# Divided weights, x in quarters, queries blanked to 128 rows: one edit of a two-block transformer kernel on one Trainium2 core

## The chip, the core and the metric

The kernel runs on one core of one Trainium2 chip. A core has five engines that work side by side: PE (TensorE, matrix products), DVE (VectorE, elementwise work and sums), ACT (ScalarE, functions of one operand with a scale), POOL (GpSimd) and SP (SyncE, which here issues the DMAs). Each runs its own instructions in order; semaphores hold one engine back until another has done something. Products land in PSUM, everything else lies in SBUF. The metric is the time of one execution on the device in microseconds (us); noise is small: the runs of this kernel lie within 0.02% of each other.

## The reference

Two blocks follow each other, both on 256 tokens of width 1024, float32. Cut to what matters:

```python
def first_block(x, ...):
    h = x + 0.5 * swiglu(rmsnorm(x, ffn1_norm), ffn1_w_gu, ffn1_w_down)
    u = rmsnorm(h, mix_norm)
    qa, ka, va, qb, kb, vb, qi, ki, wi, g = split(u @ w_in)      # 8 + 8 heads of 64
    qa, ka, qb, kb = (rmsnorm(z, its gain of 64) for z in (qa, ka, qb, kb))
    out_a = dsa_attention(qa, ka, va, qi, ki, wi, bias_dsa)      # the 64 best keys
    out_b = moba_attention(qb, kb, vb, bias_moba)                # one block of 256: causal
    g_a, g_b = split(sigmoid(g + b_gate))
    h = h + (g_a * (out_a @ w_branch_dsa) + g_b * (out_b @ w_branch_moba)) @ w_out
    return h + 0.5 * swiglu(rmsnorm(h, ffn2_norm), ffn2_w_gu, ffn2_w_down)

def second_block(x, mem, ...):                                   # two layers
    for i in range(2):
        a = rmsnorm(h, norm_mix[i])
        h = h + (mla_mixer(a) if i == 0 else stick_breaking_mixer(a))
        h = h + mem_cross_attn(rmsnorm(h, norm_cross[i]), rmsnorm(mem, norm_mem[i]))
        h = h + square(relu(rmsnorm(h, norm_mlp[i]) @ w_in)) @ w_out
    return rmsnorm(h, norm_final)

def mem_cross_attn(h, m, w_q, w_kv, w_o):                        # 4 heads of 128, 256 keys
    p = softmax(q @ k.T * 128 ** -0.5)
    return (p @ v) @ w_o
```

The mla mixer has 8 causal heads: scores contract 128 + 64 numbers, values have 128. Its output also goes through a softmax whose sum can be divided out before or after the product with the values.

## The kernel before, in words

**Products.** Each float32 factor is split into a high part, which one pass of PE takes exactly, and a low part. `mm3` makes one product of three matmuls, L394 (high by high), L395 and L396 (each with one low part). Weights stream in chunks by SP's DMAs into a ring of four buffers `w_raw`; ACT writes a chunk's high part `whi` (L351), DVE the low part `wlo` (L359), and a chunk is used once PE has waited for both (`take_chunk`). `next_hi(n)` and `next_lo(n)` split the chunk four places on in the plan, so ACT and DVE stand at most a ring ahead of PE.

**Phases.** A list of phases is walked by each engine in the same order: ffn1, the projections of the first mixer, its attention (`Attend`), mixture, ffn2, mla down, up, attend and out, a norm phase, the memory attention (`CrossAttention`), mlp, the second mixer (sb_in, stick, sb_out), and norm, memory attention, mlp and the final norm again. The order inside of a phase is written out by hand.

**A norm** before a projection is not applied to the rows: x is transposed on PE (L428) in four pairs of 128 columns, ACT writes the pair's high part `xt_h` with the gain (L441), DVE the low part `xt_l` (L494), and the root of the mean square, found meanwhile by ACT (L450) and DVE (L469 to L478), scales the outcome later. `norm_tensor`, `norm_scalar` and `norm_vector` do two pairs (one half) each.

**The opening.** x lands in three pieces (256, 256 and 512 columns) between the first chunks. Chunk 0, two tiles of 512 columns, is split tile by tile (L367, L374), chunks 1 to 3 whole. PE transposes pairs 0 and 1, multiplies with chunk 0, transposes pairs 2 and 3, and goes on with chunks 1, 2 and 3 (`up`), chunk c holding k = 2c and 2c + 1, two row tiles t each. L773 is the product of gate and up that frees the accumulator.

**Attention.** `Attend` works in groups of up to 512 score columns. For each, PE multiplies queries and keys (`score`, L1353), DVE adds the bias and finds the negated maximum (`log_vector`, L1450), ACT takes exp with the row's sum (L1430), PE transposes the weights (`turn`, L1362), DVE copies them (`copy_vector`, L1439), PE multiplies with the values (`value`, L1373). At the end of a row tile `out_rows` (DVE, L1299, L1300) divides by the sum, `fin.turn` (PE, L1312) transposes the rows, and `take_hi`, `take_lo` (L1325) split them for the next projection. Fillers stand between the groups: for the first mixer the gates' products, for mla the memory's keys and values (`keys0`, `values0`); their `groups` say after which group each step stands. In the first mixer two heads of 64 share the 128 partitions of `qt` and `kt`; a score matmul takes the half of one head, and a group holds heads of the same half:

```python
half = slice(64 * (hd % 2), 64 * (hd % 2) + 64)
qk=[(qt[half, k4, t * P:(t + 1) * P], kt[half, k4, 0:keys])]
```

`CrossAttention` has the same steps for 4 groups, in an order of its own, between the queries' projection and `project` (the output's). `memory` makes it, and `mem_groups` its groups.

**Tails.** `tail_scalar` and `tail_vector` order, at the end of an output projection, the splits of the coming chunks, the residual's additions and the following norm. A feed-forward network has the same in its own `tail`, and `Project` copies a unit's outcome out of PSUM (`copy_out`, L1000 for sb).

## Time and profile before

| | us |
|---|---|
| median of 3 runs | 1296.85 (1296.83 to 1296.98) |
| the profiled execution | 1297.06 |
| its span on the core | 1295.2 |
| PE busy | 1267.4 (98%) |
| DVE busy | 761.2 (59%) |
| ACT busy | 651.4 (50%) |

The span runs from the first to the last recorded instruction; the 1.86 around it are start and end of the program. The granted clock of TensorE over the span was 0.998 of full speed. Rows of the timeline further below name an engine, a line of the kernel, the operation with its output and input, shapes, and in brackets how long the engine was idle before and which work of another engine ended that. Runs of like instructions are one row, whose start is that of the first and whose time is busy time. Matmul records overlap: a matmul of 512 columns is busy for 0.39 but the next starts 0.23 later, so costs are read from starts.

### The profile page before, as it was taken

What the parts mean: (1) busy time and instruction counts of PE and PEld (TensorE: products, weight loads), DVE (VectorE), ACT (ScalarE), POOL (GpSimd) and SP (SyncE); (2) the same over time, 40 slices, a digit from 0 to 9 for tenths busy, and PEclk for the clock granted to TensorE, in tenths of its full rate; (3) what the DMA queues carried; (4) which work ended last, traced back from release to release, by engine and by line L of the source; (5) the groups of instructions that cost most, each with busy time, mean ns of one, the idle gap of its engine ahead of it and who ended that gap; (6) DMA issues with size and microseconds to landing.
All of it is one profiled execution on the core that took longest, in us unless ns stands there. A gap on an engine that the chain in (4) does not pass through costs nothing.

```text
span 1295.2 us, 16841 instructions
## 1 busy us (share of the span) xinstructions
PE 1267.4 (98%) x6766; PEld 1084.2 (84%) x6766; DVE 761.2 (59%) x1089; ACT 651.4 (50%) x836; POOL 18.1 (1%) x22
## 2 busy tenths in 40 slices
PE   8999999999999999999999999999999999999997
PEld 6888888888888888888888799999787887889896
DVE  6554548887676555448755575554644655754544
ACT  6454447564355444437945464443555744643432
POOL 0000000001000000000000000000000000000001
PEclk9999999999999999999999999999999999999999
DMA  8755546544443655534723175554474332655540
GB/s 289 284 192 183 187 144 231 210 147 153 157 147 133 221 189 196 188 133 152 267 70 126 66 257 183 181 193 130 164 258 163 109 103 82 224 199 182 192 131 33
DMA packets 39213, 221.72 MB, mean 171 GB/s; under 512 B 4485, under 2 KB 5141, under 8 KB 23648
## 3 DMA queue, kind: packets, MB, share of 16 engines
q1 hardware_dynamic: 36672, 214.20, 47.8%
q0 software_dynamic: 1024, 4.22, 1.0%
q10 hardware_dynamic: 1440, 2.22, 0.7%
q8 instruction: 54, 0.88, 0.3%
q14 instruction: 23, 0.19, 0.0%
HBM read 219.55 MB, written 1.07 MB: 170 GB/s over the span
## 4 chain that ended last, share of the span: by engine, by line
PE 88%; DVE 7%; ACT 3%; issue 1%; DMA 1%; SPq 0%; ACTq 0%; DVEq 0%
PE ps L394 22%; PE ps L396 22%; PE ps L395 22%; PE ps L603 4%; PE ps L605 4%; PE ps L604 4%; DVE wlo L359 3%; PE ps L1353 2%; PE ps L1373 2%; ACT whi L351 1%; PE ps L955 1%; PE ps L1362 1%; PE ps L428 1%; PE ps L636 1%; ACT xt_h L441 1%
## 5 line engine op out<-in xcount | busy, mean ns | idle before, releaser
L359 DVE TENSOR_TENSOR wlo<-w_raw,whi 128x2048 fp32r<-128x2048 f32 (+4 forms) x244 | 468.3, 1927 | 381.6 <-ACT whi L351 381.2
L351 ACT ACTIVATE whi<-w_raw 128x2048 fp32r<-128x2048 f32 (+4 forms) x244 | 393.4, 1618 | 427.5 <-PE ps L396 323.4
L394 PE MATMUL ps<-whi,xt_h 128*128 128x512 f32 (+3 forms) x784 | 308.5, 394 | 4.9 <-DVE xt_l L494 1.7
L396 PE MATMUL ps<-whi,xt_l 128*128 128x512 f32 (+3 forms) x784 | 302.8, 386 | 0.0
L395 PE MATMUL ps<-wlo,xt_h 128*128 128x512 f32 (+3 forms) x784 | 302.2, 385 | 0.0
L394 PE MATMUL ps<-whi,ot_h 128*128 128x512 f32 x594 | 235.7, 397 | 0.5 <-DVE ot_l L785 0.5
L396 PE MATMUL ps<-whi,ot_l 128*128 128x512 f32 x594 | 232.1, 391 | 0.0
L395 PE MATMUL ps<-wlo,ot_h 128*128 128x512 f32 x594 | 231.8, 390 | 0.0
L394 PEld LDWEIGHTS ps<-whi,xt_h 128*128 128x128 f32 x784 | 147.3, 188 | 38.6 <-issue 8.0
L396 PEld LDWEIGHTS ps<-whi,xt_l 128*128 128x128 f32 x784 | 147.2, 188 | 29.4
L395 PEld LDWEIGHTS ps<-wlo,xt_h 128*128 128x128 f32 x784 | 147.5, 188 | 27.1
L603 PE MATMUL ps<-xt_h,whi 128*128 128x256 f32 x512 | 145.6, 284 | 3.2 <-DVE xt_l L494 1.8
L605 PE MATMUL ps<-xt_l,whi 128*128 128x256 f32 x512 | 145.2, 284 | 0.0
L604 PE MATMUL ps<-xt_h,wlo 128*128 128x256 f32 x512 | 145.2, 284 | 0.0
L396 PEld LDWEIGHTS ps<-whi,ot_l 128*128 128x128 f32 x594 | 111.6, 188 | 23.7
L394 PEld LDWEIGHTS ps<-whi,ot_h 128*128 128x128 f32 x594 | 111.7, 188 | 22.7 <-issue 1.2
L395 PEld LDWEIGHTS ps<-wlo,ot_h 128*128 128x128 f32 x594 | 111.8, 188 | 21.5
L603 PEld LDWEIGHTS ps<-xt_h,whi 128*128 128x128 f32 x512 | 98.3, 192 | 4.9 <-issue 4.4
L604 PEld LDWEIGHTS ps<-xt_h,wlo 128*128 128x128 f32 x512 | 98.3, 192 | 0.5
L605 PEld LDWEIGHTS ps<-xt_l,whi 128*128 128x128 f32 x512 | 98.3, 192 | 0.0
L441 ACT ACTIVATE xt_h<-ps,gain 128x256 fp32r<-128x256 f32 x88 | 34.3, 478 | 45.0 <-PE ps L428 45.0
L494 DVE SCALAR_TENSOR_TENSOR xt_l<-ps,gain,xt_h 128x256 fp32r<-128x256 f32 x88 | 36.4, 477 | 23.1 <-ACT xt_h L441 23.1
(205 smaller groups left out, 878.3 us busy)
## 6 DMA issues: line engine op xcount, KB each, us to landing
w_raw<-ffn_mid SPq DMA_DIRECT2D x80, 768.0 KB, 4.3
w_raw<-mlp_mid SPq DMA_DIRECT2D x56, 1024.0 KB, 5.0
w_raw<-w_qkv SPq DMA_DIRECT2D x12, 1024.0 KB, 5.0
w_raw<-w_sb_qkv SPq DMA_DIRECT2D x12, 1024.0 KB, 5.1
w_raw<-w_xkv SPq DMA_DIRECT2D x8, 1024.0 KB, 5.0
w_raw<-ffn_first SPq DMA_DIRECT2D x8, 512.0 KB, 4.1
w_raw<-w_gate_b SPq DMA_DIRECT2D x4, 1024.0 KB, 5.0
w_raw<-w_gate_a SPq DMA_DIRECT2D x4, 1024.0 KB, 4.8
```

Source lines behind the costliest of these rows:

```text
L351: nc.scalar.activation(whi[:, s, 0:tiles * width], w_raw[:, s, 0:tiles * width], ACT.Copy).then_inc(w_hi, 1)
L359: nc.vector.tensor_tensor(wlo[:, s, 0:tiles * width], w_raw[:, s, 0:tiles * width], whi[:, s, 0:tiles * width].bitcast(F32), ALU.subtract) ...
L394: nc.tensor.matmul(acc, hi, whi[:, s, c], start=start, stop=False)
L395: nc.tensor.matmul(acc, hi, wlo[:, s, c], start=False, stop=False)
L396: return nc.tensor.matmul(acc, lo, whi[:, s, c], start=False, stop=stop)
L441: last = nc.scalar.activation(to[:, k], bank[:, j * S:(j + 1) * S], ACT.Copy, scale=gain[:, 8 * NORM[name] + k:8 * NORM[name] + k + 1])
L494: last = nc.vector.scalar_tensor_tensor(out=lo[:, k], in0=bank[:, j * S:(j + 1) * S], scalar=g, in1=hi[:, k].bitcast(F32), op0=ALU.mult, o ...
L603: nc.tensor.matmul(acc, whi[:, s, c], xt_h[:, k], start=k == 0, stop=False)
L604: nc.tensor.matmul(acc, wlo[:, s, c], xt_h[:, k], start=False, stop=False)
L605: last = nc.tensor.matmul(acc, whi[:, s, c], xt_l[:, k], start=False, stop=k == KC - 1)
L1353: last = nc.tensor.matmul(bankA[g % 2][:, head["at"]:head["at"] + head["width"]], q, k, start=i == 0, stop=i == len(head["qk"]) - 1)
L1373: last = nc.tensor.matmul(head["out"], pt[:, g % 2, c:c + P], val, start=i == 0, stop=i == len(head["v"]) - 1)
```

## The change

Seven edits, in the order of the program:

1. x lands in four quarters; chunks 0, 1 and 2 are split tile by tile (semaphores `tile_hi`, `tile_lo`); PE has an order of its own for step 0 of ffn1 (`first_tensor`): k = 2c of chunk c, the transposes of pair c + 1, k = 2c + 1 of chunk c.
2. The first mixer's queries are copied twice, with a gain column that is zero in one half (`QZ_A`, `QZ_B`), to `qt` and to `q_odd`, which lies over `ot_h` and `ot_l`. A score matmul contracts all 128 partitions, of which 64 hold zeros in the queries.
3. In mla and in the memory attentions (`turned`) DVE divides the weights by their sum (`scale_vector`) before they are transposed; the values become the stationary and the weights the moving factor, so the output stands transposed in PSUM, and `out_rows` and `fin.turn` fall away. `take_hi` and `take_lo` come one group sooner.
4. In the memory attentions (`bare`) `peak_vector`, one maximum straight from PSUM, replaces `log_vector`, and exp reads PSUM; the next score into the same bank waits for exp. Their order on all engines is written anew, both layers share their semaphores, and the norm's phase is gone: `tail_scalar` and `tail_vector` do the whole norm ahead of the last split.
5. `keys0` stands one group sooner in mla.
6. At ffn2's end the third split stands ahead of the sums and the root.
7. In sb_in's first unit ACT copies the outcome before the splits.

```diff
         def first_hi(act, n):
+            act.wait_ge(w_loaded[n], 16)
+            for tile, full in ((0, tile_hi), (1, w_hi)):
+                cols = slice(tile * TW, (tile + 1) * TW)
+                nc.scalar.activation(whi[:, n, cols], w_raw[:, n, cols], ACT.Copy).then_inc(full, 1)
...
         def tail_scalar(act, chunks, following):
             for n in chunks[:-1]:
                 next_hi(act, n)
-            if following:
-                norm_scalar(act, following, 0)
+            norm_scalar(act, following, 0)
+            norm_scalar(act, following, 1)
+            rms_scalar(act, following)
             next_hi(act, chunks[-1])
-            if following:
-                norm_scalar(act, following, 1)
...
+            def first_tensor(self, pe, c):
+                if c < 3:
+                    pe.wait_ge(tile_lo, c + 1)
+                else:
+                    take_chunk(pe, self.n0 + c)
+                    tables.tensor(pe)
+                for j, k in enumerate((2 * c, 2 * c + 1)):
+                    if j == 0:
+                        xt_ready(pe, self.name, k)
+                    elif c < 3:
+                        norm_tensor(pe, self.name, (c + 1) // 2, ((c + 1) % 2,))
+                        take_chunk(pe, self.n0 + c)
+                    for t in range(NT):
+                        last = mm3(bankA[t], xt_h[:, k, t * P:(t + 1) * P], xt_l[:, k, t * P:(t + 1) * P],
+                                   slot_of(self.n0 + c), j, TW, k == 0, k == KC - 1)
...
-                rms_scalar(act, self.following)
+                if self.following == "mla":
+                    next_hi(act, chunks.pop(2))
+                if self.following:
+                    rms_scalar(act, self.following)
...
-                    if self.name == "ffn1" and c < 2:
-                        cols = (slice(S, TW), slice(TW, D))[c]
+                    if self.name == "ffn1" and c < 3:
+                        cols = slice((c + 1) * S, (c + 2) * S)
...
+                    elif unit.odd is not None:
+                        for half, to in enumerate((unit.to[:, unit.base:unit.base + 4, s], unit.odd[:, :, s])):
+                            g = unit.gains + half
+                            last = nc.scalar.activation(to, bank, ACT.Copy, scale=gain[:, g:g + 1])
...
+                    late = self.norm == "sb" and unit.u == 0
+                    if not late:
+                        for n, _ in unit.n[:-1]:
+                            next_hi(act, n)
                     self.copy_out(act, unit)
...
             def score(self, pe, g):
                 if g >= 2:
-                    pe.wait_ge(self.logits, g - 1)
+                    pe.wait_ge(self.probs if self.bare else self.logits, self.g0 + g - 1)
...
             def turn(self, pe, g):
-                pe.wait_ge(self.probs, g + 1)
+                pe.wait_ge(self.scaled if self.turned else self.probs, self.g0 + g + 1)
...
-                        last = nc.tensor.matmul(head["out"], pt[:, g % 2, c:c + P], val,
+                        weights = pt[:, g % 2, c:c + P]
+                        left, right = (val, weights) if self.turned else (weights, val)
+                        last = nc.tensor.matmul(head["out"], left, right,
...
+            def scale_vector(self, dve, g):
+                dve.wait_ge(self.probs, self.g0 + g + 1)
+                own(dve, dve_own, nc.vector.reciprocal(rinv[:, c:c + n], rsum[:, c:c + n]))
+                nc.vector.tensor_tensor(rows, rows, rinv[:, c:c + n].unsqueeze(2).to_broadcast([P, n, width]),
+                                        ALU.mult).then_inc(self.scaled, 1)
+            def peak_vector(self, dve, g):
+                dve.wait_ge(self.scores, self.g0 + g + 1)
+                nc.vector.tensor_reduce(nmax[:, c:c + len(heads)],
+                                        bankA[g % 2][:, 0:len(heads) * width].rearrange("p (h k) -> p h k", k=width),
+                                        AX.X, ALU.max, negate=True).then_inc(self.logits, 1)
...
-                            half = slice(64 * (hd % 2), 64 * (hd % 2) + 64)
+                            q = q_odd[b][:, hd // 2] if hd % 2 else qt[:, k4]
-                                qk=[(qt[half, k4, t * P:(t + 1) * P], kt[half, k4, 0:keys])],
+                                qk=[(q[:, t * P:(t + 1) * P], kt[:, k4, 0:keys])],
...
-                            (4, 5, 6, 7, 7, None, None, 8), bankT)
+                            (3, 4, 5, 6, 6, None, None, 7), bankT)
...
-            pair_scalar(act, "ffn1", 0)
-            first_hi(act, 0)
-            first_hi(act, 1)
-            pair_scalar(act, "ffn1", 1)
-            split_hi(act, 1)
-            split_hi(act, 2)
-            norm_scalar(act, "ffn1", 1)
+            for part in range(3):
+                pair_scalar(act, "ffn1", part)
+                first_hi(act, part)
+            pair_scalar(act, "ffn1", 3)
             split_hi(act, 3)
```

`first_lo` and DVE's part of the opening mirror ACT's. Where the order of instructions moves, two places show it. First ACT in the opening, from the split of chunk 0's tiles on (`w_loaded` counts the landing of a ring buffer, `xt_ps` PE's transposes). Before:

```order
L367 ACTIVATE whi<-w_raw 128x512 [waits w_loaded0]
L367 ACTIVATE whi<-w_raw 128x512
L441 ACTIVATE xt_h<-ps,gain 128x256 [waits xt_ps]
L441 ACTIVATE xt_h<-ps,gain 128x256
L351 ACTIVATE whi<-w_raw 128x1024 [waits w_loaded1]
L351 ACTIVATE whi<-w_raw 128x1024 [waits w_loaded2]
L441 ACTIVATE xt_h<-ps,gain 128x256 [waits xt_ps]
L441 ACTIVATE xt_h<-ps,gain 128x256
L441 ACTIVATE xt_h<-ps,gain 128x256 [waits xt_ps]
L441 ACTIVATE xt_h<-ps,gain 128x256
L351 ACTIVATE whi<-w_raw 128x1024 [waits w_loaded3]
```

and now:

```order
L451 ACTIVATE xt_h<-ps,gain 128x256 [waits xt_ps]
L451 ACTIVATE xt_h<-ps,gain 128x256
L377 ACTIVATE whi<-w_raw 128x512 [waits w_loaded1]
L377 ACTIVATE whi<-w_raw 128x512
L451 ACTIVATE xt_h<-ps,gain 128x256 [waits xt_ps]
L451 ACTIVATE xt_h<-ps,gain 128x256
L377 ACTIVATE whi<-w_raw 128x512 [waits w_loaded2]
L377 ACTIVATE whi<-w_raw 128x512
L451 ACTIVATE xt_h<-ps,gain 128x256 [waits xt_ps]
L451 ACTIVATE xt_h<-ps,gain 128x256
L361 ACTIVATE whi<-w_raw 128x1024 [waits w_loaded3]
```

The copy of each pair of x stands between the splits of two chunks, where before pairs 2 and 3 came together behind chunk 2, and chunks 1 and 2 are split in two halves each.

Then PE in the first memory attention, from the transposes of the first group's weights on (`lg` the weights, `rel` keys and values, `pt` the transposed weights, `nat` the rows of the output). Before:

```order
L1362 MATMUL ps<-const,lg 128x128 [waits mem0_probs]
L1362 MATMUL ps<-const,lg 128x128 x3
L1353 MATMUL ps<-rel,qt 128x256 [waits mem0_logits,mem_q0_taken]
L1353 MATMUL ps<-rel,qt 128x256
L1373 MATMUL ps<-rel,pt 128x128 [waits mem0_p_sb,fill_copied]
L1373 MATMUL ps<-rel,pt 128x128 x3
L1362 MATMUL ps<-const,lg 128x128 [waits mem0_probs]
L1362 MATMUL ps<-const,lg 128x128 x3
L1353 MATMUL ps<-rel,qt 128x256 [waits mem0_logits]
L1353 MATMUL ps<-rel,qt 128x256
L1373 MATMUL ps<-rel,pt 128x128 [waits mem0_p_sb]
L1373 MATMUL ps<-rel,pt 128x128 x3
```

and now, from the third score on:

```order
L1399 MATMUL ps<-rel,qt 128x256 [waits mem0_probs,mem_q0_taken]
L1399 MATMUL ps<-rel,qt 128x256
L1408 MATMUL ps<-const,lg 128x128 [waits mem0_scaled]
L1408 MATMUL ps<-const,lg 128x128 x3
L1399 MATMUL ps<-rel,qt 128x256 [waits mem0_probs]
L1399 MATMUL ps<-rel,qt 128x256
L1408 MATMUL ps<-const,lg 128x128 [waits mem0_scaled,fill_copied]
L1408 MATMUL ps<-const,lg 128x128 x3
L1421 MATMUL ps<-pt,rel 128x128 [waits mem0_p_sb]
L1421 MATMUL ps<-pt,rel 128x128 x3
L1408 MATMUL ps<-const,lg 128x128 [waits mem0_p_sb,mem0_scaled]
L1408 MATMUL ps<-const,lg 128x128 x3
```

Two scores stand ahead of the second block of transposes, which wait for the division (`mem0_scaled`); the third score waits for exp (`mem0_probs`) rather than for the logits; the values (L1421) have weights and values changed about, and the transposes of rows (L1312) are gone.

## Rows read from the trace of the kernel before

**Rows 1.** The page, busy time, share of the span and instructions of each engine.

```profile
PE 1267.4 (98%) x6766; PEld 1084.2 (84%) x6766; DVE 761.2 (59%) x1089; ACT 651.4 (50%) x836; POOL 18.1 (1%) x22
```

**Rows 2.** Timeline of PE, opening: start, us, engine, line, operation, [idle before <- releaser].

```profile
8.24 0.66 PE L428 MATMUL ps<-const,h 128*128 128x128 f32 x4 [1.88 <-DMA h<-x]
8.66 0.48 PE L394 MATMUL ps<-whi,xt_h 128*128 128x512 f32 x1
...
19.29 0.50 PE L394 MATMUL ps<-whi,xt_h 128*128 128x512 f32 x1
...
22.49 0.47 PE L394 MATMUL ps<-whi,xt_h 128*128 128x512 f32 x1 [0.17 <-DVE nat L773]
```

**Rows 3.** Timeline of ACT, opening.

```profile
8.94 0.84 ACT L441 ACTIVATE xt_h<-ps,gain 128x256 fp32r<-128x256 f32 x2 [1.44 <-PE ps L428]
...
14.49 1.07 ACT L351 ACTIVATE whi<-w_raw 128x1024 fp32r<-128x1024 f32 x1
15.44 1.07 ACT L450 ACTIVATE lg<-h 128x1024 f32<-128x1024 f32 x1
```

**Rows 4.** Timeline of DVE, opening.

```profile
7.38 1.28 DVE L374 TENSOR_TENSOR wlo<-w_raw,whi 128x512 fp32r<-128x512 f32 x2
9.81 0.88 DVE L494 SCALAR_TENSOR_TENSOR xt_l<-ps,gain,xt_h 128x256 fp32r<-128x256 f32 x2 [1.15 <-ACT xt_h L441]
```

**Rows 5.** Timeline of PE, one group of the first mixer's attention.

```profile
291.30 1.00 PE L1373 MATMUL ps<-v,pt 128*128 128x64 f32 x8
292.23 1.13 PE L1353 MATMUL ps<-kt,qt 64*128 64x256 f32 x4
...
293.63 0.39 PE L395 MATMUL ps<-wlo,xt_h 128*128 128x512 f32 x1
```

**Rows 6.** Timeline of PE, mla's attention: a score block, then its end.

```profile
652.06 1.06 PE L1373 MATMUL ps<-v,pt 128*128 128x128 f32 x8
652.95 0.60 PE L1353 MATMUL ps<-kt,qt 128*128 128x256 f32 x2
...
654.91 0.40 PE L395 MATMUL ps<-wlo,xt_h 128*128 128x512 f32 x1
...
658.76 0.60 PE L1312 MATMUL ps<-const,nat 128*128 128x128 f32 x4
659.20 0.60 PE L1353 MATMUL ps<-kt,qt 128*128 128x256 f32 x2
...
663.37 0.65 PE L1312 MATMUL ps<-const,nat 128*128 128x128 f32 x4 [0.95 <-DVE nat L1300]
663.87 0.60 PE L1353 MATMUL ps<-kt,qt 128*128 128x256 f32 x2
```

**Rows 7.** Timeline of DVE, the division of mla's rows.

```profile
662.42 0.17 DVE L1299 RECIPROCAL rinv<-rsum 128x4 f32<-128x4 f32 x1
662.63 0.69 DVE L1300 TENSOR_TENSOR nat<-ps,rinv 128x512 f32<-128x512 f32 x1
```

**Rows 8.** Timeline of PE, the joints ffn2 to mla and into the second mixer.

```profile
599.28 0.38 PE L394 MATMUL ps<-whi,xt_h 128*128 128x320 f32 x1 [1.06 <-DVE wlo L359]
...
939.23 0.47 PE L394 MATMUL ps<-whi,xt_h 128*128 128x512 f32 x1 [1.31 <-ACT nat L1000]
```

**Rows 9.** Timeline of ACT ahead of the second joint.

```profile
933.01 5.51 ACT L351 ACTIVATE whi<-w_raw 128x2048 fp32r<-128x2048 f32 x3
```

**Rows 10.** Waits of PE from 700 to 745: us in total, times, the longest.

```profile
PE ps L1373 <- DVE pt L1439: 1.1, 2, 0.8
...
PE ps L1362 <- ACT lg L1430: 0.8, 1, 0.8
```

**Rows 11.** Timeline of PE, the first memory attention's end.

```profile
743.33 0.36 PE L603 MATMUL ps<-xt_h,whi 128*128 128x256 f32 x1 [0.91 <-DVE xt_l L494]
```

**Rows 12.** Timeline of ACT, the first memory attention.

```profile
718.50 0.60 ACT L2085 ACTIVATE qt<-ps 128x512 f32<-128x512 f32 x1 [0.75 <-PE ps L955]
718.99 0.50 ACT L1430 ACTIVATE lg<-lg,nmax 128x256 f32<-128x256 f32 x1
```

More of the change, by code:

```diff
@@ L285, in build @@
         ident_in = sem("ident_in")
-        x_in = [sem(f"x_in{part}") for part in range(3)]
-        first_tile = sem("first_tile")
+        x_in = [sem(f"x_in{part}") for part in range(4)]
+        tile_hi = sem("tile_hi")
+        tile_lo = sem("tile_lo")
         blanks = sem("blanks")
@@ L1317, in take_hi @@
                 t, b = self.fins[f][:2]
-                act.wait_ge(rows_ps, self.f0 + f + 1)
+                if self.turned:
+                    act.wait_ge(self.done, self.fins[f][2])
+                else:
+                    act.wait_ge(rows_ps, self.f0 + f + 1)
                 nc.scalar.activation(ot_h[:, 4 * b:4 * b + 4, t * P:(t + 1) * P],
@@ L1397, in tensor @@
                     for f, last in enumerate(self.last):
-                        if last == g - 2:
+                        if last == g - 2 and not self.turned:
                             self.fin.turn(pe, f)
@@ L1462, in vector @@
                         self.log_vector(dve, g + 1)
+                    if self.turned and g < len(self.groups):
+                        self.scale_vector(dve, g)
                     for f, last in enumerate(self.last):
                         if last == g - 2:
-                            self.fin.out_rows(dve, f)
-                        if last == g - 3:
+                            if self.turned:
+                                self.fin.take_lo(dve, f)
+                            else:
+                                self.fin.out_rows(dve, f)
+                        if last == g - 3 and not self.turned:
                             self.fin.take_lo(dve, f)
@@ L2001, in build, with __init__ @@
         class CrossAttention:
-            def __init__(self, i, fills, q_unit, groups, fins):
+            def __init__(self, i, fills, q_unit, groups, fins, like=None):
                 self.cross, self.mlp = f"cross{i}", f"mlp{i}"
@@ L2009, in __init__ @@
                 self.unit = q_unit
-                self.att = Attend(f"mem{i}", groups, fins, [])
+                self.att = Attend(f"mem{i}", groups, fins, [], turned=True, bare=True, like=like and like.att)
                 self.fin, self.keys_ready, self.values_ready = self.att.fin, fills[0].ready, fills[1].ready
@@ L2013, in __init__ @@
                 self.full = sem(f"mem_out{i}_full")
-                ends[self.n0], ends[self.n0 + 1] = (self.full, 3), (self.full, 4)
+                ends[self.n0], ends[self.n0 + 1] = (self.full, NT), (self.full, NB * NT)
             def query(self, pe, n, t, ks):
@@ L2090, in scalar @@
                 nc.scalar.preload_act_table_set("natural_log_exp_and_others")
-                next_hi(act, n0)
                 act.wait_ge(*self.q.scaled)
-                self.evacuate(act, 0)
-                self.take(act, 0)
-                self.evacuate(act, 1)
-                self.take(act, 1)
+                for t in range(NT):
+                    self.evacuate(act, t)
+                    self.take(act, t)
                 for g in range(4):
                     self.att.exp_scalar(act, g)
+                next_hi(act, n0)
                 self.fin.take_hi(act, 0)
@@ L2108, in residual @@
                 for t in range(NT):
-                    dve.wait_ge(self.full, NT * t + block + 1)
+                    dve.wait_ge(self.full, NT * block + t + 1)
                     hb = h[:, t, block * TW:(block + 1) * TW]
@@ L2504, in build, with memory @@
                          before_need=[mla_down.split_ready, mla_down.turned_ready], aside=(mem_norm(0), 1))
-        def memory(i, fills, following):
-            cross = CrossAttention(i, fills, unit("q", rows=row(f"cross{i}"), to=qt, scale=MEM_SCALE), *mem_groups())
-            return [Norm(f"cross{i}"), cross, Ffn(f"mlp{i}", 8, 4, False, 1.0, following)]
+        def memory(i, fills, following, like=None):
+            cross = CrossAttention(i, fills, unit("q", rows=row(f"cross{i}"), to=qt, scale=MEM_SCALE), *mem_groups(), like)
+            return [cross, Ffn(f"mlp{i}", 8, 4, False, 1.0, following)]
         def memory_values(i, banks, steps):
@@ L2548, in build @@
         phases += [sb_in, stick, sb_out]
-        phases += memory(1, (keys1, values1), None)
+        phases += memory(1, (keys1, values1), None, memory0[0])
         phases.append(Final(phases[-1]))
@@ L2591, in _ @@
             dve.wait_ge(consts_in, 16)
-            pair_vector(dve, "ffn1", 0)
-            first_lo(dve, 0)
-            first_lo(dve, 1)
-            pair_vector(dve, "ffn1", 1)
-            split_lo(dve, 1)
-            split_lo(dve, 2)
-            norm_vector(dve, "ffn1", 1)
+            for part in range(3):
+                pair_vector(dve, "ffn1", part)
+                first_lo(dve, part)
+            pair_vector(dve, "ffn1", 3)
             split_lo(dve, 3)
```

202 lines of the change are left out of this document (111 added, 91 removed).

## The prediction

> **What bounds the kernel now.** I read the busy shares first [rows 1]: PE is busy for 1267.4 of 1295.2 us, 98% of the span, VectorE for 59% and ScalarE for 50%. So there are two ways to save: fewer or cheaper instructions on PE, or the few microseconds in which PE waits. What VectorE and ScalarE gain or lose counts only at places where PE waits for them. Next the timeline of each such place, PE first, then the engine that it waits for: the opening [rows 2 to 4], a score block of the first mixer and one of the mla mixer [rows 5, 6], the rows' transposes at the end of mla [rows 6, 7], the two joints between phases [rows 8, 9], and the memory attention [rows 10 to 12].
>
> **The opening: +5.7.** Before, step 1 of the first feed-forward network starts at 22.49 on PE [rows 2]. The chain behind it: ScalarE's split of chunk 3 ends at 14.49 + 1.07 = 15.56 [rows 3], then the two sums of squares, the root, the split of the next chunk and the hidden row's product, together 22.49 - 15.56 = 6.93. PE itself is full until then: from 19.29 twelve matmuls, 0.17 of waiting, then step 1. The new order leaves this tail as it is, so the question is when the split of chunk 3 ends.
> Now four rounds follow each other, and each is a ring through three engines: six matmuls of k = 2c, the four transposes of x's next pair, that pair's copy on ScalarE, its low part on VectorE, the low part of the next chunk's first tile on VectorE, and only then the six matmuls of k = 2c + 2. Their prices: matmuls 0.24 each, taken from twelve in (22.3 - 19.29) = 3.0 less the slow entry and rounded to 1.45 for six; four transposes 0.65 (the group at 8.24 [rows 2]); the pair 0.04 + 0.84 (at 8.94 [rows 3]) and 0.03 + 0.88 (at 9.81 [rows 4]); the tile 1.28 / 2 = about 0.6 (at 7.38 [rows 4]); some 0.1 of hand-overs. Sum 4.6 a round, where PE's own work in it (twelve matmuls and four transposes) is 3.3-3.5: PE idles over a microsecond in each. The first matmul may start somewhat sooner than 8.66, at 8.15, since tile 0 no longer waits behind the second pair's transposes. So k = 2 starts at 12.75, k = 4 at 17.35, the last transposes end at 19.45, the pair on ScalarE at 20.3, and the split of chunk 3, 1.07 long, at 21.35. With the same tail, step 1 starts at 21.35 + 6.93 = 28.3 instead of 22.49, so **+5.7**. Before, the transposes of pairs 2 and 3 stand together ahead of a long run of matmuls, so one ring is paid where now three are. Bounds: if the tail shrinks as far as PE's own matmuls of chunk 3 allow, they end near 26.2, +3.8; if every hand-over costs 0.2 more, +6.5.
> That x lands in four quarters costs nothing in this sum: only the first wait of PE is on x (1.88 before 8.24 [rows 2]), and on SP's queue, where the last piece now stands ahead of chunk 3's load, chunk 3 is wanted by ScalarE only at 20.3, 6 us later than before.
>
> **Scores of the first mixer: -3.95.** Every group of eight value records takes 0.93 from its start to the next block where 64-row scores follow (291.30 to 292.23 [rows 5]) but 0.89 for twice as wide records where 128-row scores follow (652.06 to 652.95 [rows 6]). The four 64-row score records then take 1.40 (292.23 to 293.63, to the second matmul behind them, [rows 5]); eight records of 128 rows take 1.96 (652.95 to 654.91 [rows 6]), so four of them, at 0.216, would take 1.96 - 0.86 = 1.10. That is 0.30 on leaving, of which I leave 0.1 to the different matmul behind, so 0.195; on entering, 64-column records should cost about 0.74 and cost 0.93, again 0.195. So 0.39 for each of ten blocks whose scores stand alone, and some 0.04 for the first, where two groups follow each other: **-3.95**. Bounds: nothing, if the cost belongs to the change of shape and not of rows, and -3.95. The four added copies on ScalarE are 0.60 each at most (nearest: 128x512 (at 718.50 [rows 12])) in a phase where it waits for PE; I cost them at nothing.
> The nearest rule of the Trainium skill, TensorEngine Tiling (Array Packing), section Key Properties, says that a change of tiling mode drains TensorE; the 0.19 at each border agrees with it, and by it the whole 3.95 would come back.
>
> **Feed-forward 2 to mla: -0.8.** PE waits 1.06 at 599.28 for the low part of the third split [rows 8], which VectorE does after the root. The new order does it before. Between 0 and -1.22 (the wait and the slow restart); VectorE goes on without a gap into mla_up, where part is given back, so -0.8.
>
> **Mla's end: -2.65.** With weights divided beforehand and the values stationary, the output arrives turned: four blocks of transposes go, 0.44 each (658.76 to 659.20 [rows 6]), 1.75, and so does the wait of 0.95 at 663.37, 1.12 with its slow restart [rows 6], since reciprocal and product of the rows (0.69 [rows 7] and some 0.17) no longer stand between values and turn. Instead such a product stands in each of six groups between exp and transposes. It is covered by the fills and by the next scores in all but the first; there I take 0.2. Value matmuls have equal size either way round. The key fill moves one group sooner, to groups 3 to 7, and covers the last ones. 1.75 + 1.12 - 0.2 = 2.67.
>
> **Memory attention: -1.5 each, -3.0 for two.** Removed: two blocks of transposes, 0.87; waits of 1.1 and 0.8 [rows 10]; and 0.91 ahead of the mlp at 743.33 [rows 11]: 3.7 in all. Added: the peak of a group (one 128x512 instruction, nearest 0.69 [rows 7]), then exp (two of 0.50 (at 718.99 [rows 12])), then division (0.86), a chain of 2.5 before the first transposes, and the third score waits for exp as well, while PE has only scores and one turn of the queries to do, some 1.5: waits of 1.1 at the third score, 0.5 at the first transposes, 0.5 at the next and 0.1 later, 2.2 in sum, all on PE, where everything else queues behind them. -1.5. Bounds: 0 and -3.7. The second is taken to be the same.
>
> **Second mixer's joint: -1.4.** PE waits 1.31 at 939.23 for ScalarE's copy [rows 8], which stands behind three splits of 5.51 together [rows 9]. The new order copies first. The splits then are 1.25 late at most, and next is a chunk that PE reaches some microseconds later. Bounds -1.4 and 0.
>
> **Tail of the output projections.** The second half's norm and root now precede the last split, and the separate norm phase goes. No wait stands there in the rows and none is seen to come: 0.
>
> **Sum**: +5.7 - 3.95 - 0.8 - 2.65 - 3.0 - 1.4 = -6.1. The profiled execution took 1297.06 for a span of 1295.2, the median is 1296.85; 1296.85 - 6.1 = 1290.7.
>
> **Rivals.**
> 1. The opening costs nothing: ScalarE and VectorE run ahead and the ring closes behind PE's own 3.3. Against it: ring 4.6 by rows, and the transposes can't be issued sooner. 1285.0. Chance 7%.
> 2. The division is exposed: six times 0.86 in mla, less the 0.2 counted, +5.0, and the memory attentions give nothing, +3.0: 1298.7, within 0.2% of before. For it: VectorE was the one waited for there. Against: fills of several microseconds lie between. 8%.
> 3. The other side, slower: 64-row score matmuls of the two halves of the array run in pairs, and blanking them to 128 rows doubles their time. Twelve blocks of 0.86 net, half of which would be saved now: +5.2 instead of -3.95, 1299.9. It decides if the net time of four 64-row records is nearer 0.43 than 0.86; the row at 292.23, 1.13 busy [rows 5], has them one after the other, since a group holds heads of one half only. 5%.
> The same page of the Trainium skill, section Theoretical Speedup, gives up to twice the speed for contractions of 64 rows or fewer; by it this change would lose time. The trace does not show it for a block that stands alone.
> 4. Blanking gives nothing: the loss at a block's edges is of another kind. 1290.7 + 3.95 = 1294.6, -0.17%. 5%.
> The forecast with its own spread: 75%.
>
> **Chances and range.** A measurement of this kernel can tell some 0.2%, 2.6 us, from no change. Faster by more: the forecast and rival 1, 82%. Within: rivals 2 and 4, 13%. Slower: rival 3, 5%. The range leaves out rivals 1 to 3, 20%, and reaches from 1286.5, where the opening costs 3.8 and the memory attentions give 4 between them and mla more, to 1294.8, rival 4 and the dear opening.
>
> **What would show it.** Right: step 1 of the first network starts on PE near 28, with idle of over 1 us ahead of k = 2, 4 and 6; 128-row score records of the mixer leave at 1.1 instead of 1.40; no wait at the joints of 599 and 939 (both shifted); transposes of rows are gone in mla, with no wait over 0.3 between its groups; the memory attention has two or three waits of 0.4 to 1.1 for ScalarE or VectorE and none ahead of the mlp. Wrong: PE without idle time in the opening, or waits of 0.5 or more ahead of every transpose block in mla, or a wait that goes from one joint to the next split. The opening is the term that I trust least: a miss of 1 us in it is more than the joints hold.

## The result and the profile after

| | before | changed |
|---|---|---|
| median of 5 runs, us | 1296.98 | 1289.62 |
| lowest to highest | 1296.83 to 1297.42 | 1288.85 to 1290.51 |
| ratio, 95% interval | | 0.9943 (0.9929 to 0.9958) |
| profiled execution / its span | 1297.06 / 1295.2 | 1288.85 / 1287.0 |

The change makes the kernel 7.4 us faster; 6.1 had been forecast. The profiled execution is the fastest of the five, and 8.2 faster than that of before. The five runs of the changed kernel lie 1.7 us apart, those of before 0.6. That small spread of before, and the 0.02% of its first three runs, is not all of its noise: 44 further runs of it, taken beside the experiments, lie between 1296.26 and 1298.66, with medians of 1297.04 to 1297.13.

PE's transposes for the norms (L428 before, L438 after) are good milestones, since they stand in both kernels. The distance between them says where the time went. A milestone is the start of the first transpose of a norm's second half; for cross0, cross1 and the memory's norm it is the very first transpose. Behind the opening, a stretch that no edit touches repeats within 0.15 us in all kernels of this study. The first stretch does not: without the new opening it took 200.25 to 200.75 in seven profiled executions, in which PE's first weight matmul started at 8.20 to 8.68.

| stretch | before | changed | difference |
|---|---|---|---|
| start to the mixer's norm (opening, ffn1) | 200.75 | 206.28 | +5.53 |
| to ffn2's norm (first mixer) | 203.14 | 199.51 | -3.63 |
| to mla's norm (ffn2) | 187.05 | 187.03 | 0 |
| to the memory's norm (joint, mla down) | 25.19 | 24.00 | -1.19 |
| to cross0's norm (mla) | 82.12 | 79.58 | -2.54 |
| to mlp0's norm (memory attention) | 48.04 | 45.58 | -2.46 |
| to sb's norm (mlp0) | 182.39 | 182.41 | 0 |
| to cross1's norm (second mixer) | 131.19 | 129.77 | -1.42 |
| to mlp1's norm (memory attention) | 48.04 | 45.59 | -2.45 |
| to the end | 187.32 | 187.30 | 0 |

The opening of the changed kernel, on PE (start, us busy, engine, line, operation, idle before and its releaser), answers to [rows 2]:

```profile
8.06 0.50 PE L404 MATMUL ps<-whi,xt_h 128*128 128x512 f32 x1 [1.31 <-DVE wlo L384]
...
12.59 0.51 PE L404 MATMUL ps<-whi,xt_h 128*128 128x512 f32 x1 [1.04 <-DVE wlo L384]
...
14.11 0.60 PE L438 MATMUL ps<-const,h 128*128 128x128 f32 x4
...
17.15 0.51 PE L404 MATMUL ps<-whi,xt_h 128*128 128x512 f32 x1 [1.05 <-DVE wlo L384]
...
28.00 0.47 PE L404 MATMUL ps<-whi,xt_h 128*128 128x512 f32 x1 [1.81 <-DVE nat L800]
```

Two rounds are 12.59 - 8.06 = 4.53 and 17.15 - 12.59 = 4.56 long, with over 1 us idle in each, and step 1 starts at 28.00 instead of 22.49. On ScalarE, [rows 3] become these: the last pair's copy, then the split of chunk 3, whose end moved from 15.56 to 21.09.

```profile
19.30 0.84 ACT L451 ACTIVATE xt_h<-ps,gain 128x256 fp32r<-128x256 f32 x2 [2.67 <-PE ps L438]
20.03 1.06 ACT L361 ACTIVATE whi<-w_raw 128x1024 fp32r<-128x1024 f32 x1
```

One group of the first mixer, with 128 rows, answers to [rows 5]:

```profile
296.35 1.00 PE L1421 MATMUL ps<-v,pt 128*128 128x64 f32 x8
297.19 1.08 PE L1399 MATMUL ps<-kt,q_odd_b 128*128 128x256 f32 x4
...
298.34 0.39 PE L405 MATMUL ps<-wlo,xt_h 128*128 128x512 f32 x1
```

From the values to the scores it takes 0.84 (0.93 before), from the scores to the second matmul behind them 1.15 (1.40): 0.09 and 0.25 less, 0.34 a group. In the first memory attention PE waits at these three places, in place of the waits of [rows 10] and the 0.91 of [rows 11]:

```profile
718.29 1.10 PE L1399 MATMUL ps<-rel,qt 128*128 128x256 f32 x4 [0.82 <-ACT lg L1480]
719.23 0.60 PE L1408 MATMUL ps<-const,lg 128*128 128x128 f32 x4
...
721.07 0.63 PE L1408 MATMUL ps<-const,lg 128*128 128x128 f32 x4 [0.37 <-DVE lg L1492]
...
722.97 0.66 PE L1408 MATMUL ps<-const,lg 128*128 128x128 f32 x4 [0.23 <-DVE lg L1492]
```

The first block of transposes, at 719.23, follows the scores without a wait. The division that it needs, on VectorE, was done at 718.38 + 0.69 = 719.07:

```profile
718.38 0.69 DVE L1492 TENSOR_TENSOR lg<-lg,rinv 128x512 f32<-128x512 f32 x1
```

### The profile page after: what moved, and what is told of

Read it like the earlier page. It is cut to its first block, busy times and chain, and to the rows that moved or that the text cites. A ratio compares the mean times of both kernels' runs of the same rounds, so it can differ in the third digit from the quotient of the medians.

```text
span 1287.0 us, 16779 instructions
## 1 busy us (share of the span) xinstructions
PE 1260.3 (98%) x6736; PEld 1081.3 (84%) x6736; DVE 763.9 (59%) x1079; ACT 652.7 (51%) x842; POOL 18.1 (1%) x22
## 4 chain that ended last, share of the span: by engine, by line
PE 88%; DVE 7%; ACT 3%; issue 1%; DMA 0%; ACTq 0%; DVEq 0%
PE ps L404 22%; PE ps L406 22%; PE ps L405 22%; PE ps L631 4%; PE ps L630 4%; PE ps L629 4%; DVE wlo L369 3%; PE ps L1399 2%; PE ps L1421 2%; PE ps L438 1%; PE ps L987 1%; ACT whi L361 1%; PE ps L1408 1%; PE ps L662 1%; ACT xt_h L451 1%
```

## Experiments

Names with a_ are versions of the changed kernel, with b_ of the kernel before. The kernel before ran again beside each of them, and each ratio is to those runs. The last column is the stretch of the table above that the edit touches, in us, from the trace; except in the first three rows it is free of what the opening does.

| kernel | median (range), us | ratio to before (95%) | stretch touched |
|---|---|---|---|
| a_oldopen | 1283.37 (1282.76 to 1283.45) | 0.9894 (0.9879 to 0.9909) | opening, ffn1 200.71 |
| a_early | 1283.36 (1283.30 to 1283.52) | 0.9895 (0.9880 to 0.9910) | opening, ffn1 200.74 |
| a_best | 1283.22 (1283.09 to 1283.76) | 0.9892 (0.9877 to 0.9907) | opening, ffn1 200.73 |
| b_blank | 1293.29 (1292.96 to 1293.60) | 0.9971 (0.9960 to 0.9982) | first mixer 199.56 |
| b_dummy64 | 1300.81 (1300.29 to 1302.07) | 1.0030 (1.0019 to 1.0042) | first mixer 206.82 |
| b_dummy128 | 1294.09 (1293.35 to 1294.32) | 0.9975 (0.9966 to 0.9985) | first mixer 200.32 |
| a_mlarows | 1297.21 (1296.09 to 1299.62) | 1.0004 (0.9995 to 1.0014) | mla 86.78 |
| a_mlakeys | 1292.20 (1292.03 to 1293.31) | 0.9962 (0.9947 to 0.9977) | mla 82.37 |
| a_keys | 1291.44 (1290.81 to 1292.07) | 0.9956 (0.9939 to 0.9973) | mla 81.39 |
| a_memold | 1294.32 (1293.71 to 1295.62) | 0.9980 (0.9970 to 0.9989) | memory 48.03, 48.08 |
| a_memlog | 1292.49 (1291.61 to 1293.11) | 0.9962 (0.9947 to 0.9977) | memory 46.74, 46.74 |
| a_joints | 1292.05 (1291.65 to 1292.97) | 0.9962 (0.9947 to 0.9977) | joints 25.13, 131.18 |

### The opening: a_oldopen, a_early, a_best

a_oldopen takes the opening back whole:

```diff
-            for part in range(3):
-                pair_scalar(act, "ffn1", part)
-                first_hi(act, part)
-            pair_scalar(act, "ffn1", 3)
+            pair_scalar(act, "ffn1", 0)
+            first_hi(act, 0)
+            first_hi(act, 1)
+            pair_scalar(act, "ffn1", 1)
+            split_hi(act, 1)
+            split_hi(act, 2)
+            norm_scalar(act, "ffn1", 1)
             split_hi(act, 3)
```

> The changed kernel with the opening of before (x in three pieces, only chunk 0 split by tiles, the old order on PE, ScalarE and VectorE). Theory (the new opening costs 5.5 us, a ring of 4.57 a round against PE's own 3.3, and nothing later gives it back): step 1 of ffn1 starts on PE at 22.5 instead of 28.0, and the time is 1289.6 - 5.5 = 1284.1. Rival (the later start is partly taken up by waits for weights further on, which the old opening would meet again): 1286 or more, with new waits of PE in ffn1 behind 22.5.

a_early keeps quarters and tiles, and moves only PE's transposes (twelve, of pairs 1 to 3, each pair one place or two ahead):

```diff
             def first_tensor(self, pe, c):
+                if c == 0:
+                    norm_tensor(pe, self.name, 0, (1,))
                 if c < 3:
                     pe.wait_ge(tile_lo, c + 1)
...
                     elif c < 3:
-                        norm_tensor(pe, self.name, (c + 1) // 2, ((c + 1) % 2,))
+                        if c < 2:
+                            norm_tensor(pe, self.name, 1, (c,))
```

> The changed kernel with only the place of x's transposes on PE moved: pairs 0 and 1 before the first matmul, pair 2 between k = 0 and k = 1, pair 3 between k = 2 and k = 3; quarters and tiles stay. Theory (the cost is the ring: six matmuls stand in it ahead of each pair's transposes): pair 3's copy on ScalarE ends near 13.8, the split of chunk 3 near 14.9, step 1 starts near 21.8, and the time is 1289.6 - 6.2 = 1283.4. Rival (the cost lies in splitting by tiles and landing x in quarters, which is kept): step 1 stays near 28 and the time near 1289.6.

Both came out at 1283.4: 6.3 below the changed kernel's median, and 5.5 in the traces. Step 1 in a_early:

```profile
13.13 0.60 PE L438 MATMUL ps<-const,h 128*128 128x128 f32 x4
...
22.47 0.47 PE L404 MATMUL ps<-whi,xt_h 128*128 128x512 f32 x1 [0.91 <-DVE nat L803]
```

So the whole loss is the place of the transposes; quarters and tiles cost nothing, and gain nothing over the old opening either (22.47 against 22.49). The start is 0.7 later than I expected of a_early: the split of chunk 3 ran from 14.49 to 15.55, just as in [rows 3], where I had expected its end near 14.9, and the tail behind it took 6.92. The rival that puts the loss down to tiles and quarters falls. a_oldopen's rival, by which part of the gain is lost again further on, falls too: in both kernels all stretches behind the opening repeat the changed kernel's.

Step 1 of a_early waited 0.91 for the tail. a_best moves half of the tail forward:

```diff
                 first_hi(act, part)
+            rms_scalar(act, "ffn1", range(1))
             pair_scalar(act, "ffn1", 3)
```

> The kernel with the early transposes, and ScalarE's sum of squares of the first row tile put into its idle 1.3 us ahead of the last pair's copy. Theory (step 1 waited 0.9 on PE for the chain of sums, root, split and product): the root ends 0.9 sooner, step 1 starts at 21.7 instead of 22.47, 1283.36 - 0.8 = 1282.6. Rival (the last pair's copy is late by it, PE's own matmuls end later): 1283.4 or more.

```profile
12.69 1.05 ACT L460 ACTIVATE lg<-h 128x1024 f32<-128x1024 f32 x1
13.64 0.19 ACT L460 ACTIVATION_READ_ACCUMULATOR lg<-h 128x1 f32 x1
14.18 0.84 ACT L451 ACTIVATE xt_h<-ps,gain 128x256 fp32r<-128x256 f32 x2 [0.34 <-PE ps L438]
```

```profile
8.24 0.66 PE L438 MATMUL ps<-const,h 128*128 128x128 f32 x4 [1.33 <-DMA h<-x]
...
22.46 0.47 PE L404 MATMUL ps<-whi,xt_h 128*128 128x512 f32 x1 [0.55 <-DVE nat L804]
```

The step still started at 22.46, not at 21.7, and 1283.2 is the rival's time and not the 1282.6 of my theory. The sum of squares fitted into ScalarE's gap, and VectorE's split, which the product stands behind, began at 19.51 instead of 20.17. But in this execution x's second quarter held PE until 8.24 (7.50 in a_early's), and PE's last matmul ahead of step 1 started at 21.53 instead of 21.18; idle time of PE fell from 0.91 to 0.55. VectorE's product now waits for ScalarE's operand, and that one for PE:

```profile
21.33 1.10 ACT L732 ACTIVATE lg<-ps,rs 128x256 f32<-128x256 f32 x2 [2.96 <-PE ps L406]
```

```profile
21.84 1.11 DVE L804 SCALAR_TENSOR_TENSOR nat<-ps,rs,lg 128x256 f32<-128x256 f32 x2 [0.57 <-ACT lg L732]
```

So in this execution PE's work from the second quarter on is the bound. What a_best would give where the quarter lands as early as in a_early's, no trace shows; the times of the three kernels overlap, and I take them for one result.

### Blanked queries: b_blank, b_dummy64, b_dummy128

b_blank is edit 2 on the kernel before, and nothing else: the second copy of the queries and the scores over 128 rows.

> The kernel before with the blanked queries alone. Theory (a block of 64-row score matmuls that stands alone between 128-row ones pays 0.2 on entering and 0.2 on leaving, ten blocks): 1297.0 - 3.6 = 1293.4, with a ratio of 0.9972. Rival (64-row matmuls of two halves run side by side): 1302 or more. Second rival (no difference between shapes; the mixer's gain of the change came from elsewhere): 1297.0.

The stretch of the first mixer falls from 203.14 to 199.56, -3.58: the whole of the changed kernel's -3.63. The rival with pairs side by side is out by 9 us. Is the price one of the shape or of the border? The two next kernels put one more transpose of 128 rows between the score matmuls of a group, in 64-row form and in 128-row form:

```diff
-                for head in self.groups[g]:
+                for n, head in enumerate(self.groups[g]):
+                    if self.select and len(self.groups[g]) == 2 and n == 1:
+                        nc.tensor.transpose(bankA[g % 2][:, head["at"]:head["at"] + P], ident, ident)
```

> The kernel before with one more 128x128 transpose of the identity, written into the second head's place ahead of its scores, between the two score matmuls of each of the first mixer's eight groups of two heads; the second score overwrites it. Theory (the price is paid at each border between 64-row and 128-row matmuls): two more borders a group, 0.39, beside 0.11 to 0.22 of the transpose itself: +8 x 0.5 to 0.6 = +4 to +4.8, 1301 to 1301.8. Rival (the price belongs to each 64-row matmul, not to borders): only the transpose, +0.9 to +1.8, 1297.9 to 1298.8.

> The blanked queries on the kernel before, and the same added transpose between the two score matmuls of eight groups. Theory (price at the borders between 64-row and 128-row matmuls): no borders are left, so only the transpose costs, 8 x 0.11 to 0.22: 1293.3 + 0.9 to 1.8 = 1294.2 to 1295.1. Rival (the added transpose costs 0.5 by itself, wherever it stands, as it cost beside 64-row scores): 1293.3 + 4 = 1297.3.

A group with 64 rows, in b_dummy64:

```profile
292.24 0.70 PE L1355 MATMUL ps<-kt,qt 64*128 64x256 f32 x2
292.86 0.33 PE L1353 MATMUL ps<-const 128*128 128x128 f32 x1
293.12 0.70 PE L1355 MATMUL ps<-kt,qt 64*128 64x256 f32 x2
293.75 0.50 PE L394 MATMUL ps<-whi,xt_h 128*128 128x512 f32 x1
```

and with 128 rows, in b_dummy128:

```profile
291.50 0.65 PE L1370 MATMUL ps<-kt,q_odd_b 128*128 128x256 f32 x2
291.99 0.27 PE L1368 MATMUL ps<-const 128*128 128x128 f32 x1
292.10 0.60 PE L1370 MATMUL ps<-kt,q_odd_b 128*128 128x256 f32 x2
292.34 0.58 PE L403 MATMUL ps<-whi,xt_h 128*128 128x512 f32 x1
```

The same transpose costs 0.26 to its successor's start in the one (292.86 to 293.12) and 0.11 in the other, and the scores ahead of it 0.62 and 0.49. In sum it costs 206.82 - 203.14 = 3.68, 0.46 for each of eight groups, in 64-row form, and 200.32 - 199.56 = 0.76, 0.095 a group, in 128-row form. The difference, 0.365 for an entry and an exit together, is what a block of its own costs: ten blocks of it are 3.65, measured 3.6. The Trainium skill, TensorEngine Tiling (Array Packing), section Key Properties, says that changing the tiling mode drains TensorE; the trace agrees, with 0.365 us for a pair of borders here. The same page of the Trainium skill, section Theoretical Speedup, gives up to twice the speed for 64 rows. In this kernel a group has heads of one half only, and no time was lost by giving the 64-row form up.

### Mla: a_mlarows, a_mlakeys, a_keys

a_mlarows takes `turned=True` from mla's `Attend` (the diff's edit 3 undone there), a_keys puts `keys0` back to (4, 5, 6, 7, 7, None, None, 8), a_mlakeys does both.

> The changed kernel with mla's rows divided and transposed behind the values again, as before (the memory attentions keep the divided weights). Theory (four blocks of transposes and one wait went): +2.65, 1292.3, with the wait of about 1 us at the first row tile back. Rival (the division of the weights costs VectorE and PE in each group, and the gain is from elsewhere): 1290.5 or less.

It cost 7.2 us in mla's stretch (86.78) and 7.6 in the median, not 2.65: my theory was wrong. PE waits at new places:

```profile
664.11 0.50 PE L404 MATMUL ps<-whi,xt_h 128*128 128x512 f32 x1 [1.47 <-DVE ot_l L1366]
...
672.10 0.50 PE L404 MATMUL ps<-whi,xt_h 128*128 128x512 f32 x1 [1.47 <-DVE ot_l L1366]
...
686.58 0.66 PE L1350 MATMUL ps<-const,nat 128*128 128x128 f32 x4 [1.91 <-DVE nat L1340]
```

The first two stand ahead of the key fill, whose place in PSUM is that of the output: with rows turned afterwards the output is taken one group later, and the early fill runs into it. The third is the division ahead of the last rows' transposes: the early fill has been used up by then and no longer stands between them and the last values. So I tried the fill late, with and without the turned output.

> The changed kernel with mla's rows as before and the key fill as late as before. Reverting the rows alone had cost 7.6 rather than 2.65, with two waits of 1.5 on PE ahead of the fill's steps for the low part of the rows (rows_lo), which the fill's place in PSUM waits for. Theory (the fill can stand one group sooner only since the output is taken one group sooner; with the fill late the rows cost what the trace gave): 1289.6 + 2.65 = 1292.3, no wait on PE for the rows' low part. Rival (dividing the weights gives 7.6 by itself): 1297.

> The changed kernel with the key fill as late as before, alone. Theory (the early fill is no gain by itself; it keeps the distance between fill and output): 1289.6 to 1290.2, with at most 0.5 of new waiting ahead of the transposes of group 3. Rival (without the fill ahead of the transposes of group 3, division and exp are exposed there): a wait of 1 to 2 on PE, 1291 to 1291.6.

a_mlakeys is as forecast: 1292.2, and 82.37 in its stretch against 82.12 before, with the old wait back (the waits of PE from 640 to 710: us in total, times, the longest):

```profile
PE ps L1350 <- DVE nat L1340: 1.0, 1, 1.0
```

a_keys is the rival's: +1.81 (81.39), one wait on PE for the division, that the early fill covers in the changed kernel:

```profile
660.77 0.59 PE L1399 MATMUL ps<-kt,qt 128*128 128x256 f32 x2
...
663.47 0.66 PE L1408 MATMUL ps<-const,lg 128*128 128x128 f32 x4 [1.67 <-DVE lg L1492]
```

VectorE's queue says why: the division of group 3 stands behind the logits of group 4, and these wait for PE's scores.

```profile
661.83 0.42 DVE L1511 CUSTOM_DVE_ANT_0 lg<-ps,const 128x256 f32<-128x256 f32 x1 [0.56 <-PE ps L1399]
...
662.53 0.16 DVE L1491 RECIPROCAL rinv<-rsum 128x2 f32<-128x2 f32 x1
662.72 0.69 DVE L1492 TENSOR_TENSOR lg<-lg,rinv 128x512 f32<-128x512 f32 x1
```

So the division is exposed at the one place where no fill stands between a score and the next transposes: 0.7 for the logits ahead of it (661.83 to 662.53) and 0.9 for itself. Edits 3 and 5 belong together: the turned output alone is worth 82.37 - 81.39 = 1.0, with the early fill 82.37 - 79.58 = 2.8, and the early fill alone costs 86.78 - 82.37 = 4.4.

### Memory attention: a_memold, a_memlog

a_memold has `CrossAttention`, the tails and the norm's phase of before, with the semaphores still shared; a_memlog keeps all but the maximum:

```diff
-                self.att = Attend(f"mem{i}", groups, fins, [], turned=True, bare=True, like=like and like.att)
+                self.att = Attend(f"mem{i}", groups, fins, [], turned=True, like=like and like.att)
...
-                att.peak_vector(dve, 0)
-                att.peak_vector(dve, 1)
+                att.log_vector(dve, 0)
+                att.log_vector(dve, 1)
```

> The changed kernel with the memory attentions, their tails and the norm's phase as before. Theory (each gave 2.45 in the trace: 3.7 removed, waits of 1.4 instead of 2.2 added, and the rest ahead of the norm): +4.9, 1294.5. Rival (part of this came from the earlier split chunks and would stay): 1292.5.

> The changed kernel whose memory attentions keep the divided weights and their new order, but copy the logits out of PSUM with log_vector as before (two instructions and two reads of the accumulator a group) instead of one maximum; the score into the same bank waits for the logits, not for exp. Theory (what the new form saves on VectorE, some 0.25 a group, stands in the chain from score to division once or twice, but the bank is free 1 us sooner): the wait of 0.8 ahead of the third score goes and the transposes wait for the division instead; the same within 0.5 for two layers, 1289.1 to 1290.1. Rival (the maximum is what made the term 2.45 rather than 1.5): +1.9, 1291.5.

a_memold: +2.45 and +2.5 in the two stretches, +4.7 in the median, as expected. Its waits from 700 to 760 are those of [rows 10] and [rows 11] again:

```profile
PE ps L1424 <- DVE pt L1503: 1.1, 2, 0.8
PE ps L631 <- DVE xt_l L504: 0.9, 1, 0.9
PE ps L1411 <- ACT lg L1483: 0.8, 1, 0.8
```

a_memlog: my theory of "the same within 0.5" falls; the rival comes out, if lower in the traces (+1.16 a layer, 2.3 in all) than in the median (2.9, of which the opening has a part, below). For the same stretch, a_memlog's waits and then the changed kernel's:

```profile
PE ps L1408 <- DVE lg L1492: 2.5, 3, 1.0
```

```profile
PE ps L1399 <- ACT lg L1480: 0.8, 1, 0.8
...
PE ps L1408 <- DVE lg L1492: 0.6, 2, 0.4
```

Three waits of the transposes, 2.5 in all, against 1.4. So of the 2.46 that a memory attention gives, 1.16 are those of the maximum with exp reading PSUM, which a_memlog takes back together. The other 1.30 belong to the turned output, the new order and the tails, which no run separates.

### The joints: a_joints

```diff
-                if self.following == "mla":
-                    next_hi(act, chunks.pop(2))
...
-                    late = self.norm == "sb" and unit.u == 0
-                    if not late:
-                        for n, _ in unit.n[:-1]:
-                            next_hi(act, n)
+                    for n, _ in unit.n[:-1]:
+                        next_hi(act, n)
```

(and VectorE's mirror of the first).

> The changed kernel with the splits at ffn2's end and in the second mixer's first unit in their old places. Theory (each wait is a joint of its own): +1.05 + 1.45 = +2.5, 1292.1, with waits of about 1.1 and 1.3 back on PE. Rival (the waits were side effects of the old order elsewhere): 1289.6.

Both waits are back, with +1.13 and +1.41 in their stretches; each joint stands for itself. From 590 to 640, and from 900 to 960:

```profile
PE ps L404 <- DVE wlo L369: 1.1, 1, 1.1
```

```profile
PE ps L404 <- ACT nat L1026: 1.3, 1, 1.3
```

## Why the prediction was right, point by point

**The sum.** By the trace: +5.53 - 3.63 - 1.19 - 2.54 - 4.91 - 1.42 and nothing elsewhere, -8.2; forecast +5.7 - 3.95 - 0.8 - 2.65 - 3.0 - 1.4 = -6.1. Against the median it is -7.4. Every sign was right, and each term but the tails' was tested by undoing it. The miss against the median, 1.3, is smaller than the one against the trace, 2.1, and that is luck: the memory attentions gave 1.9 more than I counted, and something that I had not forecast took 0.8 back.

**Opening, +5.7: right.** The ring of 4.6 measured 4.53 and 4.56, k = 2 at 12.59 (12.75), k = 4 at 17.15 (17.35), step 1 at 28.00 (28.3). The tail's 6.93 measured 28.00 - 21.09 = 6.91. a_early shows that the transposes' place alone makes it. Rival 1 is out. What I had not seen is a second price, below.

**Scores, -3.95: right, a little high.** An entry and an exit together cost 0.365, not 0.39, by the pair of added transposes. My even split of it was wrong: in the group shown above entering gave back 0.09 and leaving 0.25, since eight value records took 0.84 and not the 0.74 that I had worked out. Rivals 3 and 4 are out: b_blank alone gave 3.6.

**Joint to mla, -0.8: low.** I took some of the 1.22 to be given back in mla_up; only 0.03 was (-1.19). That VectorE had no gap there did not mean that PE would wait for it. **Second mixer's joint, -1.4: right** (-1.42).

**Mla, -2.65: right in size, wrong in one clause.** I costed the key fill's move at nothing and named it only as a cover. In fact, 1.8 of the 2.54 hang on it: without it the division is exposed once, 1.67. Rival 2 (the division exposed in every group) is true in its mechanism, at a place without a fill, and there costs 1.7; in the changed kernel PE has no wait between 640 and 710.

**Memory attention, -3.0: the term that failed in size.** It gave 4.91. Of the 0.96 a layer that I was short, 0.8 is the new waits: I had 1.1 + 0.5 + 0.5 + 0.1 = 2.2, the trace has 0.82 + 0.37 + 0.23 = 1.42. The step most at fault is the "0.5 at the first transposes": PE's third score block ran from 718.29 to 719.23, the division was done at 719.07, and PE did not wait there at all. I added the two waits as if each stood by itself, though PE's work behind the first covers the second.

**The tail of the projections, 0: not separated** from the memory attentions by any run; it is within their 2.46.

**Against the median** the terms would give -8.2, and 7.4 was measured. The missing 0.8 is most likely the clock's, by the last section; the runs without a trace don't show it.

## What to carry to other kernels

In this kernel, with PE busy for 98%, the one change of order that cost time put PE's own work inside the ring that it waits for. Transposes that feed the next round belong ahead of the matmuls of this one, and moving twelve of them was worth 5.5 us here. A work item that hides a chain (the key fill) is part of the edit that made the chain longer: cost the two together, and undo them together. Alone, the early fill costs 4.4 here and the turned output gives only 1.0 of the 2.8. Here a block of 64-row matmuls that stands alone between 128-row ones was cheaper by 0.36 us with its rows filled up by zeros.

The best version of this study is the changed kernel with the old opening or with the early transposes: 1283.4 (1283.2 in a_best), 13.7 below the kernel before and 6.3 below the changed one.

## What was new about the hardware

In some executions the new opening has a second price. TensorE's granted clock from 30 to 35 us, in the changed kernel's profiled execution and in that of a_joints, which has the same opening (columns: stretch, its length, busy time of PE, PE's weight loads, VectorE, ScalarE and GpSimd, granted clock, DMA share, GB/s):

```profile
30.00:35.00 5.00, 5.00 (x26) 4.11 (x25) 4.26 (x3) 3.16 (x4) 0.51 (x1) 1.00 1.00 323
```

```profile
30.00:35.00 5.00, 5.00 (x20) 4.01 (x19) 3.31 (x2) 2.11 (x3) 0.51 (x1) 0.75 0.95 329
```

and a_joints' matmuls there, 0.43 from start to start until 32.48 and 0.23 from then on:

```profile
31.20 0.63 PE L404 MATMUL ps<-whi,xt_h 128*128 128x512 f32 x1
31.63 0.63 PE L405 MATMUL ps<-wlo,xt_h 128*128 128x512 f32 x1
32.05 0.59 PE L406 MATMUL ps<-whi,xt_l 128*128 128x512 f32 x1
32.48 0.40 PE L404 MATMUL ps<-whi,xt_h 128*128 128x512 f32 x1
32.71 0.40 PE L405 MATMUL ps<-wlo,xt_h 128*128 128x512 f32 x1
```

That is the lower of the clock's two levels, 1.2 instead of 2.4 GHz, for eight matmuls, some 1.6 us in all, after an opening in which PE had idled 1.0, 1.0, 1.8 and 1.8. Of seven profiled executions with that opening, five have such a run of seven or eight slow matmuls (at 24 to 33 us) and two, the changed kernel's and a_keys', have none; none of the seven with another opening has one.

What it costs depends on where it falls. I count from PE's first weight matmul, which starts between 7.65 and 8.47, to the mixer's norm. This takes 198.22 in both executions without slow matmuls. In a_memold, a_memlog and a_joints they begin at 28 to 29, behind the last idle time, and it takes 199.76 to 199.78: the loss is 1.55. In a_mlakeys and a_mlarows they begin at 24, ahead of the last idle time, and it takes 198.35 and 198.53: the loss is only 0.1 to 0.3, since that idle time shrinks from 1.8 to 0.4 and 0.5:

```profile
28.73 0.47 PE L404 MATMUL ps<-whi,xt_h 128*128 128x512 f32 x1 [0.54 <-DVE nat L800]
```

This is the likely reason that the runs of the changed kernel lie 1.7 apart while those of a_early lie 0.2 apart, and that the median is short of the trace's 8.2; the start of the first matmul may have a part in both. The runs without a trace tell only a mean clock over the whole span: 0.998 in the changed kernel's fastest, 0.997 in its other four. That is a weak sign, since the mean takes in the last microseconds, in which PE has no more work and the clock is low in every trace. The kernel before is perhaps not free of it either: of its 44 further runs seven took 1297.9 or more, and six of these show 0.997, and none of the rest. The Trainium skill, TensorE: Matmul & The Clock Gate, section What's actually happening, has the gate follow how busy PE has been recently; the traces agree as far as they go, since ahead of PE's last matmul the clock fell only in the opening with these idle times. Why one execution of the same opening is struck and another isn't, no run here shows.

The second thing is small. In the changed kernel's memory attention a maximum over 128x512 straight from PSUM took VectorE 0.69 a group. In a_memlog the logits with a running maximum took two instructions of 0.42, 0.35 apart, with a read-out of 0.08 behind each.
